# Attention operands on 128 rows, latent attention with its heads in pairs, and constant products behind the modulation sums, in a kernel of two transformer blocks

## What is computed

```python
def _modulate(x, shift, scale):
    return _rms(x) * (1 + scale) + shift

def _fox_attention(q, k, v, log_f):       # one of five branches, H = 4, Dh = 64
    logits = (jnp.einsum('bqhd,bshd->bhqs', q_blk, k) * scale
              + jnp.moveaxis(c_blk, 1, 2)[..., None] - cum_s[:, :, None, :])
    ...
def _mla_mixer(h_lat, h_ctx, cos, sin, w_in, q_norm, kv_norm, w_uq, w_ukv, q_gain, k_gain, w_out, ...):
    def queries(cq, rotate):
        q = (_rms(cq) * q_norm) @ w_uq
        q = _rms(q.reshape(*q.shape[:2], MLA_HEADS, MLA_QK)) * q_gain      # MLA_QK = 64 + 32
        return _rope_tail(q, cos, sin) if rotate else q
    def keys_values(ckv, k_rope, rotate):
        ukv = ((_rms(ckv) * kv_norm) @ w_ukv).reshape(..., MLA_HEADS, MLA_NOPE + MLA_V)   # 64 + 64
        k_nope, v = ukv[..., :MLA_NOPE], ukv[..., MLA_NOPE:]
        k = _rms(jnp.concatenate([k_nope, k_rope_for_all_heads], axis=-1)) * k_gain
        return (_rope_tail(k, cos, sin) if rotate else k), v
    cq_l, ckv_l, kr_l = _split_cols(h_lat @ w_in, (MLA_Q_LORA, MLA_KV_LORA, MLA_ROPE))    # 512, 256, 32
    ckv_c, kr_c = _split_cols(h_ctx @ w_in[:, MLA_Q_LORA:], (MLA_KV_LORA, MLA_ROPE))
    ...
    y_lat = _block_attention(queries(cq_l, True), k_all, v_all) @ w_out
```

## Time and profile before

| | us |
|---|---|
| median of three runs | 3997.36 |
| lowest, highest | 3987.57, 4011.06 |
| profiled execution, its own time | 3997.59 |
| its span in the trace | 3996.3 |

### The profile page before, as it was taken

One profiled execution on the slowest core, in us unless ns is written; L12 is line 12 of the kernel. 1 busy time (PEld: TensorE's weight loads), 2 busy tenths in 40 slices (PEclk: granted clock), 3 DMA queues, 4 the chain that ended last, 5 costly groups with the idle time before them and its releaser, 6 DMA issues.

```text
span 3996.3 us, 44584 instructions
## 1 busy us (share of the span) xinstructions
PE 3590.3 (90%) x17294; PEld 2763.4 (69%) x17294; DVE 1721.3 (43%) x3284; ACT 1237.0 (31%) x2092; POOL 908.4 (23%) x395
## 2 busy tenths in 40 slices
PE   5998999999899898999797768999998879998998
PEld 3765776676756677666575457888886637876887
DVE  3228324432236523533488343422354375544233
ACT  2323323322323332332322422222333234533322
POOL 2112121122302221023123001222453000013443
PEclk9989989999999898999898779999999799999999
DMA  3332112122342121113111001111231020012221
GB/s 145 132 142 80 39 57 77 52 94 97 134 181 88 54 67 67 55 59 113 60 53 64 5 0 43 59 64 64 84 128 63 20 71 1 1 43 69 95 97 67
DMA packets 86468, 288.10 MB, mean 72 GB/s; under 512 B 9840, under 2 KB 20592, under 8 KB 85232
## 3 DMA queue, kind: packets, MB, share of 16 engines
q1 hardware_dynamic: 85248, 275.40, 20.4%
q10 hardware_dynamic: 1008, 9.83, 0.7%
HBM read 281.01 MB, written 4.19 MB: 71 GB/s over the span
## 4 chain that ended last, share of the span: by engine, by line
PE 51%; DVE 10%; ACT 2%; issue 1%; POOL 0%; DMA 0%; ACTq 0%; DVEq 0%; POOLq 0%
PE psum L290 13%; PE psum L291 12%; PE psum L292 12%; PE psum L293 12%; DVE psum L2332 3%; PE psum L2988 1%; PE psum L1028 0%; PE psum L2966 0%; DVE mla_q L2862 0%; DVE x L3304 0%; DVE ml_weights L2617 0%; DVE h_low L516 0%; DVE rounded_ctx L504 0%; DVE sum_k L2937 0%; DVE mla_q L2886 0%
## 5 line engine op out<-in xcount | busy, mean ns | idle before, releaser
L378 POOL TENSOR_TENSOR weights_low<-weights_loaded,weights_high 128x1024 fp32r<-128x1024 f32 (+2 forms) x377 | 897.4, 2380 | 3019.3 <-ACT weights_high L360 2954.8
L291 PE MATMUL psum<-h_high,weights_high 128*128 128x512 f32 (+1 forms) x2384 | 924.3, 388 | 69.8 <-DVE h_low L516 26.2
L292 PE MATMUL psum<-h_low,weights_high 128*128 128x512 f32 (+1 forms) x2384 | 898.1, 377 | 0.0
L293 PE MATMUL psum<-h_high,weights_low 128*128 128x512 f32 (+1 forms) x2384 | 895.5, 376 | 0.0
L291 PEld LDWEIGHTS psum<-h_high,weights_high 128*128 128x128 f32 x2384 | 461.4, 194 | 178.7 <-issue 82.4
L360 ACT CAST weights_high<-weights_loaded 128x1024 fp32r<-128x1024 f32 (+2 forms) x377 | 391.1, 1037 | 529.1 <-PE psum L293 495.6
L292 PEld LDWEIGHTS psum<-h_low,weights_high 128*128 128x128 f32 x2384 | 462.0, 194 | 87.3 <-issue 9.6
L293 PEld LDWEIGHTS psum<-h_high,weights_low 128*128 128x128 f32 x2384 | 460.5, 193 | 84.5
L291 PE MATMUL psum<-weights_high,h_high 128*128 128x512 f32 (+4 forms) x480 | 162.6, 339 | 45.2 <-ACT mixed_features L2282 22.3
L3297 DVE TENSOR_TENSOR act_low<-ffn_act,act_high 128x512 fp32r<-128x512 f32 (+1 forms) x66 | 139.9, 2119 | 142.5 <-ACT act_high L3276 142.3
L291 PE MATMUL psum<-act_high,weights_high 128*128 128x512 f32 (+1 forms) x528 | 188.7, 357 | 10.1 <-DVE act_low L3297 10.1
(11 more groups left out here) (382 smaller groups left out, 5242.4 us busy)
## 6 DMA issues: line engine op xcount, KB each, us to landing
weights_loaded<-stream_dram SPq DMA_DIRECT2D x480, 512.0 KB, 3.4
weights_loaded<-stream_dram SPq DMA_DIRECT2D x81, 128.0 KB, 3.2
weights_loaded<-stream_dram SPq DMA_DIRECT2D x12, 384.0 KB, 3.1
weights_loaded<-stream_dram SPq DMA_DIRECT2D x8, 272.0 KB, 2.8
x<-x_dram SPq DMA_DIRECT2D x1, 2048.0 KB, 9.2
arena_mem<-mem_dram ACTq DMA_DIRECT2D x2, 1024.0 KB, 6.9
x<-x_dram ACTq DMA_DIRECT2D x1, 2048.0 KB, 8.3
x_kept_dram<-x ACTq DMA_DIRECT2D x1, 2048.0 KB, 6.6
```

Source lines behind the costliest of these rows:

```text
L291: pe.matmul(out, a.high, b.high, start=start, stop=False)
L292: pe.matmul(out, a.high, b.low, start=False, stop=False)
L293: return pe.matmul(out, a.low, b.high, start=False, stop=stop)
L378: pool.tensor_tensor(self.low[s][:, 0:size], raw[:, 0:size], self.high[s][:, 0:size], ALU.subtract).then_inc(*g.event("weights_low").up(po ...
```

## The change

**Zero rows.** The queries of each head of the first block, and the mLSTM's, go into a tile of 128 rows of their own, in which the other head's half is zero (written once by GpSimd: event `zeroed`). The logits then contract over all 128 rows, against the pair's keys. An evacuation of two heads' queries becomes two instructions of 64 partitions; fox's decay rows become four ops for two.

**Ring.** `NRAW` goes from 6 to 5.

**Constant products.** Behind the sums of each of the four modulations of the second block stand 24 products of 128 columns of `ones` by `ident`; nothing reads their bank.

**Latents and up.** ckv and kr are projected first, as one group of three 128-column units over all 768 tokens (kr's 32 columns repeated four times, with features as rows), then cq 0, sums of ckv, six transposes of kr, cq 1 to 3. In `up`, all ukv units stand ahead of uq, grouped by heads; ScalarE copies q as well as squaring it; the gain is folded into tables of sines and cosines, and VectorE rotates four query tiles at once in six ops. The context's modulation stands ahead of the latent tokens', and the fences behind the latents, up and the heads are gone: heads wait for the event of their group.

**Heads in pairs.** Units go (pair, query tile, head of the pair). Features are 96 rows without zeros, in four buffers. Weighing is done once for a pair: v is the stationary operand, the turned probabilities move (128 columns), and the two heads write partitions 0 to 63 and 64 to 127 of one bank by column tiles. Two more products spread the inverse sums over 64 rows; ScalarE copies these, VectorE multiplies. The result already has the layout of the projection, so the 32 transposes and their copies go; the splits of finished pairs stand between the last pair's units.

```diff
-NRAW = 6
+NRAW = 5
...
+def busy_tensor(g, key, turn, n):
+
+    pe, S = g.pe, g.event
+    key = ("busy", key)
+    i = g.claim(key, turn.next(1))
+    for j in range(n):
+        done = pe.matmul(g.banks(i)[:, 0:P], g.ones, g.ident, start=True, stop=True)
+    done.then_inc(*S("drained").up(pe, key))
...
-        done = mm(g, out, q[rows, h // 2, at], keys_of(u, h)[rows, :], True, extra is None)
+        done = mm(g, out, q[:, h, at], keys_of(u, h), True, extra is None)
...
+def pair_of(q, j):
+    return tuple(q[HD * i:HD * (i + 1), 2 * j + i, :] for i in range(2))
...
     for n in norms:
         sums_tensor(g, n, turn)
+    busy_tensor(g, norms[-1].key, turn, 24)
...
-            copy_scalar(g, k, t.ml_q[:, j, :], g.wide(k))
+            for i in range(2):
+                half = slice(ML_QK * i, ML_QK * (i + 1))
+                for m in g.after(act, S("projected").at(k), S("zeroed").at("ml_q")):
+                    act.wait_ge(*m)
+                act.copy(t.ml_q[half, 2 * j + i, :], g.wide(k)[half, :]).then_inc(*S("drained").up(act, k))
...
-    for name, tile, value in (("up", t.up[:, :, :], 0.0),
+    for name, tile, value in (("ml_q", t.ml_q[:, :, :], 0.0), ("up", t.up[:, :, :], 0.0),
...
-                        done = mm(g, g.wide(k, x0, x1), t.ml_k[rows, h // 2, kb * P:(kb + 1) * P],
-                                  t.ml_q[rows, h // 2, x0:x1], True, True)
+                        done = mm(g, g.wide(k, x0, x1), t.ml_k[:, h // 2, kb * P:(kb + 1) * P], t.ml_q[:, h, x0:x1],
+                                  True, True)
...
-UNITS = [(h, q) for h in range(H) for q in range(QT)]
+PAIRS = H // 2
+UNITS = [(2 * pair + i, q) for pair in range(PAIRS) for q in range(QT) for i in range(2)]
...
+                pe.matmul(g.banks(7)[MLA_V * i:MLA_V * (i + 1), 0:P], t.vt[:, kb, UNITS[n][0], :],
+                          t.mla_turned[(2 * n + part) % 6][:, (kb % 3) * P:(kb % 3 + 1) * P], start=kb == 0,
+                          stop=kb == TT - 1, tile_position=(0, MLA_V * i))
...
+            done = pe.matmul(g.banks(7)[MLA_V * i:MLA_V * (i + 1), P:2 * P], inverse, g.ident, start=True, stop=True,
+                             tile_position=(0, MLA_V * i))
...
-    norms = modulations(g, 1, "mla", g.t.mla, 0, 1, latent_first=True)
+    norms = modulations(g, 1, "mla", g.t.mla, 0, 1)
```

More of the change, by code:

```diff
@@ L662, in rope_vector @@
         *S("drained").up(dve, (key, "partner")))
-    for m in g.after(dve):
-        dve.wait_ge(*m)
-    dve.tensor_tensor(out, tmp[:, :], raw[:, :], ALU.add).then_inc(*S("roped").up(dve, key))
+    for part, o in head_halves(out):
+        for m in g.after(dve):
+            dve.wait_ge(*m)
+        dve.tensor_tensor(o, tmp[part, :], raw[part, :], ALU.add).then_inc(*S("roped").up(dve, key))
 def tables_vector(g):
@@ new lines, in queries @@
+    def queries(j):
+        project_wide(g, ("mla_cq", j), turn, np.arange(j * P, (j + 1) * P), "mla_w_in_2", (0,), t.mla.h2, LATENT, each)
+    turn.i += turn.i % 2
+    for key, _ in LATENTS:
+        g.claim(key, turn.next(2), 2)
+    for part in range(KT // 2):
+        w, c = g.weights.piece(("mla_first", part), "mla_w_in_2", (0,), rows_of(2, part * 2 * P), LATENT_COLS, split=True)
+        for k in range(2):
+            kk = part * 2 + k
+            for key, at in LATENTS:
+                for lo, hi in BOTH:
+                    for m in g.after(pe, each(lo, kk)):
+                        pe.wait_ge(*m)
+                    done = mm(g, g.wide(key, lo, hi), w[:, k, at:at + P], t.mla.h2[:, kk, lo:hi], kk == 0, kk == KT - 1)
+                if kk == KT - 1:
+                    done.then_inc(*S("projected").up(pe, key))
+        if part < KT // 2 - 1:
+            done.then_inc(*S("projected").up(pe, ("mla_first", part)))
+            g.weights.used(c, "projected", ("mla_first", part))
+        else:
+            g.weights.used(c, "projected", ("mla_kr",))
@@ new lines, in gain_vector, with rotate_vector @@
+def gain_vector(g, x, heads, gain):
+    dve = g.dve
+    gb = bass.AP(tensor=gain.tensor, offset=gain.offset, ap=[[gain.ap[0][0], P], [0, heads], [1, MLA_ROPE]])
+    for m in g.after(dve):
+        dve.wait_ge(*m)
+    dve.tensor_tensor(x, x, gb, ALU.mult).then_inc(*g.event("rotated").up(dve))
+def rotate_vector(g, x, rot, tables, key):
+    dve, S = g.dve, g.event
+    even, odd = (x.rearrange("p ... (i two) -> p ... i two", two=2)[..., n] for n in range(2))
+    sin_even, sin_odd, cos_even, cos_odd = tables
+    a, b = rot
+    for out, one, two, op in ((a, even, sin_even, ALU.mult), (b, odd, sin_odd, ALU.mult),
+                              (even, even, cos_even, ALU.mult), (even, even, b, ALU.subtract),
+                              (odd, odd, cos_odd, ALU.mult), (odd, odd, a, ALU.add)):
+        for m in g.after(dve):
+            dve.wait_ge(*m)
+        dve.tensor_tensor(out, one, two, op).then_inc(*S("rotated").up(dve, key))
@@ L2897, in up_vector @@
-    for m in g.after(dve, S("kr_squared").at(TT - 1)):
-        dve.wait_ge(*m)
-    gain_vector(g, t.kr[:, 0:CT, :], CT, g.small.k_gain_row)
+            if c == 0 and n == 1:
+                finish_keys(GROUPS - 1)
+        x = t.qt[:, :, :].rearrange("p t (h d) -> p t h d", d=MLA_QK)[:, :, c * MLA_PER:(c + 1) * MLA_PER, MLA_NOPE:]
+        half = MLA_ROPE // 2
+        tables = []
+        for k in range(4):
+            tab = t.q_tables[:, k, :]
+            tables.append(bass.AP(tensor=tab.tensor, offset=tab.offset,
+                                  ap=[[tab.ap[0][0], P], [half, QT], [0, MLA_PER], [1, half]]))
@@ L3131, in mla_out_scalar @@
 def mla_out_scalar(g, l):
-    act, S, t = g.act, g.event, g.t
-    for j in range(KT):
-        for m in g.after(act, S("projected").at(("mla_yt", j))):
-            act.wait_ge(*m)
-        act.copy(t.yt.high[:, j, :], g.bank(("mla_yt", j))).then_inc(*S("mixed_high").up(act, ("mla", j)))
+    weighted_high_scalar(g, KT - 1)
     for d in range(KT):
@@ L3141, in mla_out_vector @@
 def mla_out_vector(g, l):
[L3142 to L3147 removed]
+    weighted_low_vector(g, KT - 1)
     for d in range(KT):
```

612 lines of the change are left out of this document (315 added, 297 removed).

## The result

| | us |
|---|---|
| before, median | 3997.1 (3987.57 to 4011.06) |
| changed, median | 3903.64 (3897.8 to 3908.72) |
| ratio | 0.9763, 95% interval 0.9731 to 0.9795 |
| changed, span of the profiled execution | 3907.4, mean clock 0.948 |

The forecast was 3900 with a range from 3845 to 3965. The sum is right to 4 us, but four of its terms are off by 4 to 11 us each and cancel in part. In a later set of runs the changed kernel had a median of 3914.4 (ratio 0.9797, 0.9774 to 0.982), so a difference of 10 us between kernels of different sets says nothing by itself.

What follows compares the result with a forecast made beforehand. TensorE, busy for 90% of the span, was taken as the bound. The terms −17 −15 +18 −8 −68 −6 −4 +3 sum to −97, so 3997 − 97 = 3900 us, range 3845 to 3965.

Steps and rivals of the forecast that it cites:

- A: mLSTM scores on 128 rows: zero rows raise TensorE's clock; −17 us, range −26 to −2.
- B: First-block logits on 128 rows: fewer lone stretches of 64-row products and better clock, more evacuations; −15 us, range −22 to +4.
- C: NRAW 6 to 5: the sixth weight chunk of each burst comes late; +18 us, range +8 to +25.
- D: Four bundles of 24 constant products in the modulation gaps: projections behind start at full clock; −8 us, range −10 to 0.
- E: Latents and up in a new order, uq bound by TensorE, first logits at 3236 to 3239; −68 us, range −78 to −55.
- F: Heads in pairs: less TensorE work, but features wait for ScalarE's copy in three of four steps; −6 us, range −15 to +10.
- W: Heads: time of a pair's weighing and inverse products with column halves running beside each other; taken as 1.8 us.
- rival (3): Heads: features do not wait, since copies keep out of the way; −18 us more, 3882 us; chance 0.12.
- G: Behind the heads: the 32 transposes go and their copies are spread over the last pairs; −4 us.
- H: mLSTM gate scan: GpSimd's new ml_q zeros put it 2.7 us later, and ScalarE's half copies wait; +3 us.
- (1): Heads: column halves of weighing run one after the other, +48 us, 3948 us; chance 0.12.
- (4): Heads stay at 1.2 GHz, making the kernel slower than before; +190 us, 4090 us; chance 0.03.

## Why the prediction was right, and where it was not

**A**: right, −17 forecast and −21 measured, and its rival (zero rows don't count) fell: 0.75 against 0.90. How busy TensorE is does not tell the two apart: 118 us of 150 with 64 rows in the product and with 128. Where the forecast writes 1.2 GHz, the traces have a granted clock of 0.50, half of full speed; they give no frequency.

**B**: −17 to −26 for −15, by the marks; right, if a little low, and not taken apart. Its 0.32 us for a pass of 384 columns can be read in the changed kernel, where the four products that took 1.57 us on 64 rows stand on 128 rows, two passes each:

```profile
480.54 0.86 PE L290 MATMUL psum<-arena_even,queries_even 128*128 128x384 f32 x2
481.24 0.81 PE L290 MATMUL psum<-arena_even 128*128 128x384 f32 x2
481.88 0.81 PE L290 MATMUL psum<-arena_even,queries_even 128*128 128x384 f32 x2
482.53 0.81 PE L290 MATMUL psum<-arena_even 128*128 128x384 f32 x2
```

They start 0.70, 0.64 and 0.65 us apart, so 0.32 a pass in the last two.

**C**: +19 for +18, right, though its detail was not: in the changed kernel the sixth chunk waits 1.5 to 2.1 us in ten of the bursts and not 2.9, and in the other two the fifth is late, by 3.12.

**D**: −2 to −3 for −8. The bundles fit and keep the clock (1.00 behind them, 0.50 without), but the term was sized at 2 us for each, and over the whole stretches they gave between 2.7 and less than nothing.

**E**: −67 for −68, and by its own steps: first logits 148 us behind the modulation's first projection (forecast 145 to 150), VectorE below TensorE. The sum was laid out from the new queue, so what the rope key's place does to its neighbours did not enter it.

**F**: the step that failed. Forecast −6, measured +5. W was 1.72 for 1.8, the steps with features 7.45 to 7.56 for 7.36. The step without features was "5.72 in the fourth and in the last two heads"; it takes 6.84, since I followed only the first of two copies behind the exponential. 11 steps by 1.1 us are 12 us. The sum had a slip too: 21 steps of 7.36 and 11 of 5.72 are 217.5 us and not 219.5, and without waits, as in rival (3), 21 of 6.38 and 11 of 5.72 are 197 and not 201.5. With both copies moved the steps are those of rival (3), 6.38 to 6.49 and 5.73. That the heads then take 202.5 us is near its 201.5 by chance, since some 6 us of them are the last pair's.

**G**: not there. From the last logits to the output projection it is 11 us in both kernels (3535.8 to 3546.9, 3448.9 to 3459.6). The windows, before and changed, and the end of the heads on VectorE and GpSimd in the changed kernel:

```profile
3535.80:3546.90 11.10, 9.13 (x80) 8.60 (x80) 5.48 (x13) 4.59 (x9) 0.00 (x0) 1.00 0.00 0
...
3448.90:3459.60 10.70, 8.08 (x69) 6.29 (x68) 5.84 (x12) 5.11 (x10) 0.00 (x0) 0.69 0.14 49
```

```profile
3441.64 1.77 DVE L3171 SCALAR_TENSOR_TENSOR mla_cols<-mla_cols,rstd_q 128x1 f32<-128x1 f32 x1
...
3446.15 2.64 DVE L3221 TENSOR_TENSOR mla_out_low<-mla_latents,mla_out_high 128x512 fp32r<-128x512 f32 x1 [0.87 <-ACT mla_out_high L3214]
...
3441.03 7.21 POOL L378 TENSOR_TENSOR weights_low<-weights_loaded,weights_high 128x1024 fp32r<-128x1024 f32 x3 [336.83 <-ACT weights_high L360]
```

The transposes' 3.7 us are gone, but the clock is 0.69 where it was 1.00: it is 1.00 up to 3444, and 0.63 from 3444 to 3448.9, behind waits of TensorE of 2.12 us (at 3439.22) and 1.58 us (at 3444.64). What makes these units long is in the other two views. While GpSimd splits the next three weight chunks, two instructions of VectorE take 1.77 and 2.64 us that take 0.16 and 0.69 in other units, and both stand on the chain that ends the stage; two others in that time (0.56 and 0.29) keep their length. The run with both copies first has the same pair (1.76 and 2.64), again under GpSimd's split. With VectorE's subtraction a unit later the two take 1.20 and 1.47, and the way from the last logits to the projection is 9.5 us. What each of these gives was not taken apart.

**H**: the 2.74 us wait is there as forecast; what it costs was not measured alone.

The other rivals: (1) fell with W, (3) did not come about since the features do wait, (4) fell, for the clock of the heads is 0.99, and (5) fell with E.

The 0.3 us that W has for entering and leaving was too much. Six turns of 128 columns take 0.66 us (3302.82 to 3303.48), 0.11 each, so the 28 passes of weighing and inverse would need 28 × 0.11 / 2 = 1.5 us by this estimate; they take 1.72, so entering and leaving cost no more than some 0.2 in a step. That a weigh pass of 64 columns took 0.107 us before is measured; why it did, no run shows.

So 3900 was hit with luck. Measured by the stretches, A gave 5 us more than its term, B and C together 3.5 more and the stretch behind the mLSTM stage 2 more; E with its D gave 3 less, F and G together 15 less. That makes 8 us less than forecast in the traces, and the medians moved 4.6 us more than the spans (93.5 and 88.9).

## What to carry to other kernels

When a reordering shortens TensorE's work between two uses of a bank, follow every instruction that stands behind the long one on the draining engine, not only the first: here a features copy and a turned copy both stood behind one exponential, and moving both, which costs nothing because ScalarE idled ahead of it, shortened the heads by 31 us in the traces (26 us by the medians against the one set of the changed kernel and 37 against the other). Price a stage of tiny products at the clock that it brings about (0.54 and 0.55 here, for products of 32 columns), and do not count work as saved when it is taken out ahead of a wait. And where two kernels share a stretch of code, compare stages in the traces before trusting medians that differ by a few microseconds.

## What the runs showed of the hardware

Filling the unused half of a 64-row operand with zeros raised the granted clock of a stage from 0.75 to 0.90 with the same busy time (118 of 150 us). 144 products of 32 columns, with TensorE busy all the time, went from 0.11 to 0.21 us apart, with a granted clock of 0.54 and 0.55 in their windows. 48 unread passes in a gap of 5.7 us kept the first 512-column pass behind it at 0.50 us instead of 0.79, with a granted clock of 1.00 instead of 0.50. Two column halves run beside each other when neighbours in the queue alternate between them (28 passes in 1.72 us) and hardly otherwise (2.60). VectorE instructions of 0.16 and 0.69 us took 1.77 and 2.64 while GpSimd split weights.
